# A hybrid decoder step: one chain of filling projections over all stages, and the recurrence's preparation spread over its steps

## The reference, cut to what matters

```python
def in_proj(xn, w_in, b_fgate, lb):                    # one wide projection, split into branches
    h = xn @ w_in                                      # (2048 + 8 rows) x 1024, 14 pieces of columns
def fox_prompt(q, k, v, logf): ...                     # 8 heads x 64, causal softmax with a decay term, T = 2048
def fox_sample(...): ...                               # 8 samples against 2048 paged past tokens
def hgrn2(q, k, v, logf, s0, chunk): ...               # 4 heads, state 128x128, gated linear recurrence
def mem_attn(q, mk, mv): ...                           # 4 heads x 128, 256 memory tokens
def merge_branches(...):
    mixed = sigmoid(ga) * ya + sigmoid(gb) * yb + sigmoid(gm) * ym
    return x + mixed @ w_o
```

## Time and profile before

| | |
|---|---|
| three runs | 3645.16, 3646.96, 3648.72 us (median 3646.96) |
| the profiled execution | 3645.66 us, its span 3644.1 us |
| busy | PE 81%, PEld 64%, DVE 41%, ACT 26%, POOL 16% |
| mean granted clock | 0.899 |
| DMA | 499.36 MB, 137 GB/s over the span |

### The profile page before, as it was taken

One profiled execution on the slowest core, in us unless ns is written; L12 is line 12 of the kernel. 1 busy time (PEld: TensorE's weight loads), 2 busy tenths in 40 slices (PEclk: granted clock), 3 DMA queues, 4 the chain that ended last, 5 costly groups with the idle time before them and its releaser, 6 DMA issues. The chain is left out here.

```text
span 3644.1 us, 38245 instructions
## 1 busy us (share of the span) xinstructions
PE 2951.2 (81%) x13930; PEld 2335.6 (64%) x13930; DVE 1490.2 (41%) x2774; ACT 954.3 (26%) x1806; POOL 581.9 (16%) x539
## 2 busy tenths in 40 slices
PE   4969999999239777868499999999922386799999
PEld 3847777887127565657377787778822232588887
DVE  3510001111345454553455555555556622544444
ACT  1201111111023232222244454444400110423222
POOL 2021111110252324140201002020035300000000
PEclk8979999999559898989799999999966698899999
DMA  3325422211446454534555545554366476533331
GB/s 133 104 63 160 144 67 70 70 67 51 162 152 199 150 169 144 186 121 155 168 151 148 157 130 151 150 157 138 100 211 203 129 220 193 189 114 115 120 120 47
DMA packets 304488, 499.36 MB, mean 137 GB/s; under 512 B 109028, under 2 KB 150535, under 8 KB 285607
## 3 DMA queue, kind: packets, MB, share of 16 engines
q1 hardware_dynamic: 298399, 479.43, 41.9%
q0 software_dynamic: 5904, 17.51, 1.6%
HBM read 386.18 MB, written 110.67 MB: 136 GB/s over the span
## 5 line engine op out<-in xcount | busy, mean ns | idle before, releaser
L2246 PE MATMUL hgfill_out<-hgfill_w_hi,hgfill_x 128*128 128x512 f32 x1024 | 360.4, 429 | 77.4 <-DMA hgfill_x<-x_tiles 50.9
L2246 PE MATMUL fill_out<-fill_w_hi,fill_x 128*128 128x512 f32 x1024 | 374.4, 418 | 0.0
L477 DVE TENSOR_TENSOR in_stage<-in_stage,in_out 128x512 f32<-128x512 f32 x64 | 44.0, 687 | 624.3 <-ACT in_stage L466 624.3
L2246 PEld LDWEIGHTS hgfill_out<-hgfill_w_hi,hgfill_x 128*128 128x128 f32 x1024 | 204.3, 205 | 128.2 <-issue 53.5
L823 DVE TENSOR_TENSOR fox_pt_lo<-fox_turned,fox_pt_hi 128x512 fp32r<-128x512 f32 (+1 forms) x320 | 194.9, 609 | 191.5 <-ACT fox_pt_hi L773 189.9
L773 ACT ACTIVATE fox_pt_hi<-fox_turned 128x512 fp32r<-128x512 f32 (+1 forms) x320 | 170.4, 533 | 361.2 <-PE fox_turned L728 360.6
L809 DVE CUSTOM_DVE_ANT_0 fox_probs<-fox_scores,fox_bias 128x512 f32<-128x512 f32 (+2 forms) x320 | 187.8, 609 | 108.3 <-PE fox_scores L717 66.9
L179 PE MATMUL in_out<-x_hi,in_whi 128*128 128x512 f32 x512 | 205.9, 402 | 19.8 <-POOL in_wlo L421 19.8
L466 ACT ACTIVATE in_stage<-in_out 128x512 f32<-128x512 f32 x112 | 67.0, 599 | 588.0 <-PE in_out L181 588.0
L2246 PE MATMUL hgfill_out<-hgfill_w_lo,hgfill_x 128*128 128x512 f32 x512 | 217.5, 425 | 0.0
L2246 PE MATMUL fill_out<-fill_w_lo,fill_x 128*128 128x512 f32 x512 | 212.2, 414 | 0.0
(11 more groups left out here) (374 smaller groups left out, 6141.4 us busy)
## 6 DMA issues: line engine op xcount, KB each, us to landing
hgfill_x<-x_tiles SPq DMA_DIRECT2D x64, 1024.0 KB, 5.5
fill_x<-x_tiles SPq DMA_DIRECT2D x64, 1024.0 KB, 5.4
paged_slot<-in_cache_fox_k_dram SPq DMA_DIRECT2D x128, 256.0 KB, 3.0
paged_slot<-in_cache_fox_v_dram SPq DMA_DIRECT2D x128, 256.0 KB, 3.0
mf_gate<-plain SPq DMA_DIRECT2D x96, 256.0 KB
turned<-in_stage SPq DMA_DIRECT2D x64, 256.0 KB
plain<-fill_stage SPq DMA_DIRECT2D x64, 256.0 KB, 5.4
in_raw<-in_w_in_dram SPq DMA_DIRECT2D x56, 256.0 KB, 3.1
```

The lines of the kernel that those rows point to most:

```text
L477: dve.tensor_tensor(stage[u % STAGES][:], stage[u % STAGES][:], out[u % STAGES][:], ALU.mult).then_inc(taken, 1)
L2246: ins = pe.matmul(self.out[n % self.OUTS][:], x, w, start=(k == 0 and term == 0), stop=(ends and term == 2))
```

## The change

Both Fillers are replaced by one over all eight groups (3200 matmuls), opened before the sample's work and kept until the end of `attend_memory`. Each stage takes a fixed number of its matmuls, spread evenly over the stage's slots:

```diff
+MATMULS = {"unpack": 40, "cache": 190, "sample": 170, "recur": 1750, "first": 120, "fox": 80}
...
+            fill = Filler(nc, core, inner, "fill", groups, x_tiles, x_sample_t, sample)
...
+            attend_memory(..., fill, fill.left())          # 850
```

`Filler.begin` gives a stage its slots, and SP's store of a unit moves to the slot in which the next one ends:

```diff
+    def begin(self, counts):
+        base = self.edges[-1]
+        self.edges = [base + sum(counts[:n]) for n in range(len(counts) + 1)]
...
             if not self.is_sample(n) and m + self.RING < self.first_x[-1]:
                 self.load_x(sp, m + self.RING)
-            self.store(sp, n)
+            if n >= 1:
+                self.store(sp, n - 1)
+            if n == self.units - 1:
+                self.store(sp, n)
```

The sample's stages get slots. `unpack_sample` starts the Filler (`gpsimd_start`, `gpsimd_first`, `sync_start`), takes in what `lower_bound` did (that Block is gone) and runs one slot of 40. `attend_cache` and `recur_sample` are written out without hardware loops:

```diff
+        fill.begin(fill.spread(matmuls, 2 * a.GROUPS))
+            for n, (it, s) in enumerate(order):
+                keys(it, s)
+                extra(n)
+            middle()
+            for n, (it, s) in enumerate(order):
+                values(it, s)
+                extra(a.GROUPS + n)
...
+        fill.begin(fill.spread(matmuls, B + 2))            # recur_sample; in SP's and PE's loop over samples:
+                        fill.sync(sp, 1 + b)
+                        fill.tensor(pe, 1 + b)
```

`recur_prompt` runs five filling steps ahead of its first chunk, and a unit's preparation is cut into four parts, one to a step:

```diff
+    PARTS, AHEAD = 4, 5
+        for n in range(-AHEAD, len(chunks)):
+            if n >= 0:
+                early(n)
+            if n >= 1:
+                late(n - 1)
+            if n >= BLOCK and n % BLOCK in POST_AT:
+                post(n // BLOCK - 1, POST_AT.index(n % BLOCK))
+            u, part = divmod(n + AHEAD, PARTS)
+            if u < len(units):
+                prepare(u, part)
+            extra(n)
...
-        fill = Filler(nc, core, ctx, "hgfill", *fill_with, 2 * len(chunks))
+        fill.begin(fill.spread(matmuls, 2 * (len(chunks) + AHEAD)))
```

`attend_prompt` has 120 matmuls in nine slots of its opening steps and 80 over its 640 slots, in place of 1600:

```diff
+    steps = [("fill", 0), ("set", 0)]
+    for b in range(QUADS):
+        steps += [("fill", 1 + b), ("keys", 0, b)]
...
-        fill = Filler(nc, core, ctx, "fill", *fill_with, 2 * FH * J_HEAD)
+        fill.begin(fill.spread(first_matmuls, FILLS) + fill.spread(matmuls, 2 * FH * J_HEAD))
-                fill.gpsimd_start(pool)
-                fill.gpsimd_first(pool)
```

`attend_memory` gets two slots ahead of the first tile and one after each group of pages, on every engine's walk, SP's too. The Filler's two PSUM banks are found by cutting `scores` and `turned` from two banks to one:

```diff
-        scores, turned, o_sum = psum("scores", 2), psum("turned", 2), psum("o_sum", 1)[0]
+        scores, turned, o_sum = (psum(n, 1)[0] for n in ("scores", "turned", "o_sum"))
+        fill.begin(fill.spread(matmuls, 2 * paged.GROUPS + 2))
...
             for u in range(NT + 2):
+                if u == 0:
+                    extra(0)
+                    extra(1)
...
                         keys(n // paged.SLOTS, n % paged.SLOTS)
                     elif u < NT:
                         values(n // paged.SLOTS, n % paged.SLOTS)
+                    if u < NT:
+                        extra(2 + u * PER + n % PER)
...
-                        if n >= 2:
-                            pe.wait_ge(exp_ready, n - 1)
+                        if n >= 1:
+                            pe.wait_ge(exp_ready, n)
...
-                        if n >= 2:
-                            pe.wait_ge(pt_copied, n - 1)
+                        if n >= 1:
+                            pe.wait_ge(pt_copied, n)
...
-                     lambda it, s: paged.load_group(sp, paged.v_pages, paged.GROUPS, it, s))
+                     lambda it, s: paged.load_group(sp, paged.v_pages, paged.GROUPS, it, s),
+                     lambda slot: fill.sync(sp, slot))
```

More of the change, by code:

```diff
@@ L983, in load_z, with store @@
                                  ).then_inc(z_loaded[n % 2], 16)
-                def post(blk, piece):
+                def store(blk, piece):
                     n = blk * PIECES + piece
@@ L1009, in _ @@
                     load_z(n)
-                walk(lambda u: None, lambda n: None, lambda n: None, post, extra)
+                walk(nothing, nothing, nothing, nothing, extra)
+                for piece in range(PIECES):
+                    store(BLOCKS - 1, piece)
                 sp.wait_ge(state_ready, len(chunks))
@@ new lines, in prepare @@
+                    if part == 0:
+                        dve.wait_ge(log_ready, u + 1)
+                        for c in range(CH):
+                            at = slice(c * P, (c + 1) * P)
+                            last = dve.tensor_tensor_scan(b[h][:, at], ones[:], log_f[:, at], 0.0, ALU.mult, ALU.add)
+                        last.then_inc(b_ready, 1)
+                    if part == 1:
+                        dve.wait_ge(k_ready, u + 1)
+                        dve.wait_ge(exp_ready, u * ES + 1)
+                        dve.tensor_tensor(q_run[h][:], q_run[h][:], q[h][:], ALU.mult)
@@ L1180, in post @@
                     dve.tensor_tensor(rows, rows, z[n % 2][:], ALU.mult).then_inc(rows_ready, 1)
[L1182 removed]
+                walk(prepare, weigh, advance, post, nothing)
             @block.tensor
@@ L1835, in _ @@
             def _(act):
-                a.scalar_middle(act)
-                with act.Fori(0, a.ROUNDS) as it:
-                    for s in range(a.SLOTS):
-                        a.scalar_values(act, it, s)
+                walk(nothing, lambda: a.scalar_middle(act), lambda it, s: a.scalar_values(act, it, s),
+                     lambda slot: fill.scalar(act, slot))
             @block.tensor
@@ L1925, in _ @@
                 m.then_inc(back_ready, 1)
+                fill.tensor(pe, B + 1)
+            @block.gpsimd
+            def _(pool):
+                for slot in range(fill.slots):
+                    fill.gpsimd(pool, slot)
             @block.vector
@@ L1937, in _ @@
                 link.done[0] += 1
-                with dve.Fori(0, B // 2) as it:
+                for it in range(B // 2):
                     for i in range(2):
@@ L1965, in _ @@
                 act.sem_inc(taken, 2)
-                with act.Fori(0, B // 2) as it:
+                fill.scalar(act, 0)
+                for it in range(B // 2):
                     for i in range(2):
@@ L2203, in matmuls_of, with spread, left @@
         return (len(group.tiles) - 1) * 3 * KT + KT * (5 if group.sample is not None else 3)
+    def begin(self, counts):
+        base = self.edges[-1]
+        self.edges = [base + sum(counts[:n]) for n in range(len(counts) + 1)]
+        self.slots = len(counts)
+        assert self.edges[-1] <= self.total
+    @staticmethod
+    def spread(matmuls, slots):
+        return [matmuls * (n + 1) // slots - matmuls * n // slots for n in range(slots)]
+    def left(self):
+        return self.total - self.edges[-1]
     def until(self, slot):
-        return self.total * min(slot, self.slots) // self.slots
+        return self.edges[slot]
     def group_of(self, counts, n):
```

376 lines of the change are left out of this document (191 added, 185 removed).

## The result

The changed kernel takes 3805.38 us (median of four runs, 3798.54 to 3812.84) against 3647.24 us for the kernel before beside it (3645.16 to 3648.72). The ratio is 1.0434, 95% interval 1.0408 to 1.0461: slower by 158 us. The profiled execution has a span of 3797.5 us, against 3644.1 before.

What follows compares the result with a forecast made beforehand. PE was taken to bound the prompt's attention, with 81% busy overall. Samples' stages +114, recurrence -95, prompt's attention -257 and memory attention +267 gave +29 us on 3645.7: 3675 us, range 3530 to 3780.

Steps and rivals of the forecast that it cites:

- SP's held issue: Memory attention: SP waits for PE at a unit's end before issuing the next pages; +85 in K, 66 in V.
- up to 3 us a tile, mostly under the same waits: Memory attention, V half: single `scores` bank makes the second pair wait for a maximum and two exps.
- 6 us, some 11 times: V half: PE waits for the next page group, which SP issues only after PE's slot ends; 66 us.
- Less 11 of waits for pages that stand in that half already: V half: 11 us subtracted for page waits taken to be in the kernel before.
- the lock-step: Samples' and memory stages: SP must wait for PE at unit ends before loading further, giving back gains made elsewhere.
- four times some 5 us: Cache attention: SP's next group load stands behind PE at a unit's end, four times; +20 us.
- 476 + 44 + 32: Recurrence: 64 steps of 7.4 us (476), four group changes of 11 (44), eight post pieces of 4 (32).
- the bound of -130: Recurrence: lower bound of the -95 us forecast, reached if group changes and posts are hidden.
- the chain: Prompt's attention: PE, ACT, DVE, PE dependence, uncovered without filling; 16 us a head on a base of 56.
- Rival D: Prompt's attention: PE's clock falls to a mean of 0.8, 84 us a head, +96, 3770 us; chance 0.18.
- B: Prompt's attention runs near its floor, 60 us a head, 96 us less, 3580 us; chance 0.19.
- C: Memory attention: page loads stay hidden as SP runs ahead; about 120 us, not 267; total 3530; chance 0.13.

Runs made afterwards that it cites:

- run 6: Kernel before with one bank each for scores and turned probabilities in the memory attention instead of two, filling unmoved: 3708.35 us, ratio 1.0190.
- run 4: Changed kernel with the filling's tile loads and stores issued by ACT behind its evictions instead of by SP: 3591.63 us, ratio 0.9847.
- run 1: Changed kernel with SP issuing page loads three steps ahead of the filling's transfers, memory attention only: 3649.45 us, ratio 1.0005.
- run 5: Changed kernel with page loads three steps ahead in memory and cache attention, and sample loads before the filling's transfers: 3583.93 us, ratio 0.9836.
- Run 7: Changed kernel with all four parts of a unit's preparation issued in one step of the recurrence: 3857.57 us, ratio 1.0585.

## Why the prediction was wrong

It said 3675 (3530 to 3780) with slower at 0.58. The kernel takes 3805: the direction was right, the time lies 25 us outside. The sum was +29, the spans differ by 153, so 124 us were missed. They are in the table, as what each stage took beyond its forecast: memory +114, samples +37, recurrence -33, the rest +6.

**The memory attention, +267 forecast, +381 measured, is the step that failed.** The runs take the 381 apart. Single banks without filling: 498 us against 435, +63 (run 6). Filling on top, with SP free: 652 or 653, +154 or +155 (runs 4 and 1). SP's held issue on top of that: 816, +164 or +163 (the change). The two runs that free SP agree on these sums and part within the halves:

| term, us | forecast | by run 4 | by run 1 |
|---|---|---|---|
| start | 14 | 16 | 16 |
| K: held issue | 85 | 51 | 27 |
| K: filling | 10 | 46 | 70 |
| K: single banks | 0 | 22 | 22 |
| V: held issue | 66 | 97 | 120 |
| V: filling | 103 | 108 | 85 |
| V: single banks | 0 | 41 | 41 |
| V: waits that stood there already | -11 | 0 | 0 |

- The single bank was priced at "up to 3 us a tile, mostly under the same waits", which put it at nothing. It is 63 us, 3 a tile in K and 5 in V, and hides under nothing. This is the largest error, and that sentence should have had a bound of its own.
- The filling in K was put at nothing but a group change: 10 us forecast, 46 or 70 measured, although PE is idle for much of K. (The 85 beside it counted PE's "12 to 14" us for a tile's four slots as time before the loads, so that part of the filling stands in that line.) With SP freed, what PE waits for in K of run 1 is exps (43.9 us) and the filling's tiles (37.5). My reading is that page multiplication, exps and PE's tile wait for each other in turn, so that work put in front of `score` delays all of them. No run shows it, and a rival stands beside it: with filling around them the key pages took 3.9 to 5.3 us to land, 3.0 before.
- The held issue was forecast at 14 + 85 + 66 = 165 in all, and measured at 163. The mechanism was right, the agreement of the total is luck: K was too dear and V too cheap. "6 us, some 11 times" was 110.6 us in 14 waits, 7.9 each, and PE's products behind them were slow, which the sum had left out.
- "Less 11 of waits for pages that stand in that half already" was a wrong reading: the trace has 25.6 us in three waits, and 24.0 of them are still there in run 4, with filling and SP free. Nothing was to be subtracted.

**The samples' stages, +114 forecast, +151 measured.** Of the cache attention's growth 42 us are the lock-step (126 against 84 us in runs 1 and 5), forecast 20, "four times some 5 us". Four waits of 7.0 us for pages are 27.8 of it, and PE was busy for 73.86 us where 65.85 do with pages ahead. Of the sample recurrence's 65, it is 24. The rest, 41, is filling and splits: the forecast was right to count them, but at 8 to 15 us a pair, of which I let the loads hide a part. POOL's last splits stand out behind PE's last matmul by some 17 us, where I had 12. Unpacking was +27 for +28.

**The recurrence, -95 forecast, -128 measured**, two us inside its bound. The opening came as forecast: the first chunk's products start 39 us after the stage's first load, for 40. The wait of 29.0 us for the constants began at 1158.7, while POOL still split slices in the sample recurrence; in this stage it is 7.5 us, where I had 8. POOL's first instruction of the stage, then PE's:

```profile
1180.11 0.52 POOL L1000 MEMSET hg_masks<- 128x512 f32 x1 [3.91 <-POOLq L2910]
1187.65 1.22 PE L2314 MATMUL fill_out<-fill_w_hi,fill_x 128*128 128x512 f32 x2 [29.00 <-POOLq L1016]
```

The end took 27 us for 31. What was too dear lies between: 476 + 44 + 32 = 552 us for steps, group changes and posts, against 523 from the first chunk's products to the last one's. No wait for posts is left, and the waits for splits are 29.2 us. Run 7 shows what the bound of -130 rested on: spreading alone is 53.

**The prompt's attention, -257 forecast, -254.5 measured.** 72 us a head, 578/8 = 72.2. That the number fits is luck in part, for its two parts do not: PE was busy for 60.5 us a head, where its own work was put at 55.6, and idle for 11.7, where the chain was put at 16. It is not quite the chain of the forecast either. DVE's waits for ACT's `pt_hi` were to grow; they fell. The kernel before, then the changed one:

```profile
DVE fox_pt_lo L823 <- ACT fox_pt_hi L773: 186.5, 219, 3.1
DVE fox_pt_lo L828 <- ACT fox_pt_hi L778: 69.0, 131, 1.5
```

PE waited for `pt_lo` (33.0 us in 15 waits), for exps (21.1 in 23), for keys to load (20.3 in 6, 17.0 before) and for DVE's maxima (13.8 in 30). Rival D did not come: PE was busy for 84% at a clock of 0.95. The rule of the Trainium skill that stood beside it (TensorE: Matmul & The Clock Gate, A second HAM failure mode) does not show in this stage. B fails too, and C is refuted by the 110.6 us.

**What would show it.** PE waiting for V pages "60 to 80 us": 110.6. SP waiting on `out_ready`: 243.8. K half about 270: 313. Recurrence 610 to 640: 588. 240 us for the samples' stages: 273. PE near 75% busy in the prompt's attention: 84%. DVE's waits on ACT grown: fallen. In V the waits were priced by the issue behind them and not by what PE's lower clock adds after them: PE's busy time fell from 285 to 264 us once the waits were gone.

That the bound of 150 to 310 for the memory attention, and the range of the whole with it, did not hold has one more reason: the bounds covered the lock-step and had no term for banks, and next to none for filling in K. Whether these three simply add in every mix was not tried; here they were measured one on top of the other.

## What to carry to other kernels

Where one queue serves both the stage and work woven into it, look at which wait stands ahead of which load: a wait for the consumer of step n before the load of step n + 1 makes a circle, and one step of lead breaks it. A longer lead can hold the other stream in turn, as the tiles in run 1's K half. Work moved out of a full stage into idle ones is not free there; here a matmul cost 0.17 to 0.27 us in the mean of every stage, where a dense row has 0.23, so moving many of them can win only a little, and the banks taken to make room cost 65 us by themselves. Price each resource that makes room for a change (banks, slots) by itself, with bounds, before the sum is drawn.

## What the runs showed of the hardware

- Matmuls behind idle gaps of some 7 us were slow: in the V half of the changed kernel eight value products took 4.92 to 6.50 us after gaps of 6.59 to 14.74, and 3.59 after one of 0.43. Over the half the granted clock was 0.84 with such gaps and 0.93 without.
- Short gaps do not tell the clock by themselves. With single banks and no filling, 22.5 us of waits of 1 to 2 us came with 15 us more of busy PE and 0.87 in place of 0.92 (run 6). The same two rows of waits, 14.3 and 8.1 us, stand in run 1 with filling between them, at 0.93.
- In the recurrence and the prompt's attention PE stood at 0.94 and 0.95 while idle for 10% and 16% of the time.
- The same multiply of 128x256 on DVE took 0.41 us, and 1.26 to 1.31 while POOL ran a TENSOR_TENSOR beside it (run 7). The waits do not show it, as it is busy time.
- Key pages of 256 KB took 3.0 us from issue to landing without the filling's tiles of 1 MB in the stage (median), and 3.9 to 5.3 with them (the change, runs 1 and 4).
